# A head-norm's small gate matmuls moved one step earlier and into another PSUM bank, in a two-layer transformer kernel whose TensorE queue is written out by a planner

## The reference, cut to what matters

```
h = rms_norm(x, norm_g)
q, k, v, z = split(h @ w_in, 4)                     # 1024 x 8192
q = rms_norm(q per head and map) ; k likewise       # head 64 wide, 2 maps, 16 heads
probs   = softmax(q k^T + alibi, causal)            # for each map
weights = probs[map 0] - lam * probs[map 1]
o = weights @ v                                     # 128 columns a head
o = rms_norm(o, head_norm_g) * (1 - lam_0)          # over the 128 columns of the head
o = o.reshape(b, s, 2048) * silu(z)
return x + o @ w_out                                # 2048 x 1024
```

## Time and profile before

| | |
|---|---|
| median of 3 runs | 1321.99 us (1320.73 to 1322.24) |
| the profiled execution, its own time | 1322.24 us |
| its span, from the first to the last instruction | 1320.5 us |
| mean granted TensorE clock | 0.996 |
| TensorE matmul busy | 1303.3 us, 99% |
| VectorE, ScalarE, GpSimd busy | 794.4, 612.3, 306.7 us |
| the head loop of the second layer | from about 791 us to 1286 us |

### The profile page before, as it was taken

One profiled execution on the slowest core, in us unless ns is written; L12 is line 12 of the kernel. 1 busy time (PEld: TensorE's weight loads), 2 busy tenths in 40 slices (PEclk: granted clock), 3 DMA queues, 4 the chain that ended last, 5 costly groups with the idle time before them and its releaser, 6 DMA issues.

```text
span 1320.5 us, 18425 instructions
## 1 busy us (share of the span) xinstructions
PE 1303.3 (99%) x7206; PEld 1092.6 (83%) x7206; DVE 794.4 (60%) x1568; ACT 612.3 (46%) x1299; POOL 306.7 (23%) x206
## 2 busy tenths in 40 slices
PE   7999999999999999999999999999999999999999
PEld 6877887888889999999888787888878888888787
DVE  4416564333569788877323646576767676677643
ACT  4325555333435444445314435555555565656531
POOL 4013310000037566460001412031222223131010
PEclk8999999999999999999999999999999999999999
DMA  6303332332351442342235222222222222223501
GB/s 244 96 10 103 81 95 65 97 96 96 109 210 39 154 128 70 123 129 96 65 128 198 97 88 64 97 72 72 72 80 83 94 73 72 73 72 124 203 32 64
DMA packets 110103, 130.87 MB, mean 99 GB/s; under 512 B 7488, under 2 KB 87360, under 8 KB 110016
## 3 DMA queue, kind: packets, MB, share of 16 engines
q1 hardware_dynamic: 104400, 112.39, 26.4%
q10 hardware_dynamic: 5616, 17.30, 3.5%
HBM read 120.24 MB, written 9.44 MB: 98 GB/s over the span
## 4 chain that ended last, share of the span: by engine, by line
PE 86%; DVE 6%; issue 4%; ACT 2%; POOL 1%; DMA 0%; ACTq 0%; DVEq 0%; POOLq 0%
PE ps L811 14%; PE ps L813 14%; PE ps L812 14%; PE ps L816 7%; PE ps L818 6%; PE ps L817 6%; PE ps L1018 5%; PE ps L1021 5%; PE ps L1020 5%; PE ps L1076 2%; DVE wlo L1442 2%; PE ps L1086 1%; PE ps L1058 1%; PE ps L1110 1%; PE ps L922 1%
## 5 line engine op out<-in xcount | busy, mean ns | idle before, releaser
L1442 DVE TENSOR_TENSOR wlo<-raw,whi 128x512 fp32r<-128x512 f32 (+1 forms) x290 | 235.9, 838 | 185.1 <-ACT whi L1140 184.4
L1140 ACT ACTIVATE whi<-raw 128x512 fp32r<-128x512 f32 (+2 forms) x338 | 208.5, 650 | 116.8 <-PE ps L813 91.8
L811 PE MATMUL ps<-whi,hth 128*128 128x512 f32 x592 | 243.9, 412 | 2.6 <-DVE wlo L1442 2.6
L813 PE MATMUL ps<-wlo,hth 128*128 128x512 f32 x592 | 231.6, 391 | 0.0
L812 PE MATMUL ps<-whi,htl 128*128 128x512 f32 x592 | 231.4, 391 | 0.0
L1843 POOL TENSOR_TENSOR wlo<-raw,whi 128x384 fp32r<-128x384 f32 (+1 forms) x48 | 55.7, 1179 | 421.5 <-ACT whi L1140 421.5
L811 PEld LDWEIGHTS ps<-whi,hth 128*128 128x128 f32 x592 | 111.5, 188 | 33.6 <-issue 9.2
L813 PEld LDWEIGHTS ps<-wlo,hth 128*128 128x128 f32 x592 | 111.3, 188 | 24.7
L812 PEld LDWEIGHTS ps<-whi,htl 128*128 128x128 f32 x592 | 111.8, 189 | 18.8
L1392 ACT ACTIVATE px<-px,nm 128x128 f32<-128x128 f32 (+3 forms) x128 | 70.8, 554 | 90.4 <-DVE nm L1757 87.1
L816 PE MATMUL ps<-hth,whi 128*128 128x512 f32 (+1 forms) x288 | 112.5, 391 | 0.0
(11 more groups left out here) (339 smaller groups left out, 2872.5 us busy)
## 6 DMA issues: line engine op xcount, KB each, us to landing
raw<-in_l_w_in SPq DMA_DIRECT2D x64, 512.0 KB, 4.7
raw<-in_w_gate_up SPq DMA_DIRECT2D x44, 512.0 KB, 4.9
raw<-in_w_in SPq DMA_DIRECT2D x14, 1024.0 KB, 5.4
raw<-in_w_down SPq DMA_DIRECT2D x10, 1024.0 KB, 5.0
raw<-in_l_w_out SPq DMA_DIRECT2D x8, 1024.0 KB, 5.2
raw<-in_w_in SPq DMA_DIRECT2D x24, 256.0 KB, 3.6
raw<-in_w_branch SPq DMA_DIRECT2D x8, 512.0 KB, 4.0
raw<-in_w_out SPq DMA_DIRECT2D x4, 1024.0 KB, 5.1
```

The source lines that it names most:

```text
L811: e.matmul(o, ah, wh[:, cs], start=a, stop=False)
L813: m = e.matmul(o, ah, wl[:, cs], start=False, stop=z)
L1140: return e.activation(out, in_, ACT.Copy, **how)
L1442: return e.tensor_tensor(out, src, hi_part.bitcast(F32), ALU.subtract)
```

## The change

The gate is one step now, `ga`, for all three engines. It is put one planner step earlier, behind `t2` part 0 in place of around `t2` part 1, and writes at column 0 of `b0`, the first score bank of the slot (`gate2(b)`); in slot 16 and at the end it takes a bank of its own. The bank is free after `hvar_d`, and the bank of `t2` part 1 no longer waits for it. On VectorE the reading of the sums follows the low half of `t2` part 0. The heads that wait for their gate stand in a list, `og_wait`. In `last_heads`, slot 16 starts two steps earlier and the gate of head 15 one step earlier, with its `to` where it was; the four loads of `xb` are put together, ahead of the third step of slot 15, and three of them (the first among them) wait for `og` of head 13 (`og_p` at 14). The last projection waits once for all of its four heads.

```diff
@@ -312,6 +312,7 @@
         self.block_end(1, W.dn + 10, gen, (2, 4))
         finish(gen)
         put("ab", 0)
+        self.og_wait = []
         for g in range(7):
             merge(self.proj2(g + 1), 32, self.slots(2 * g, 2 * g + 2), 14)
         merge(self.w2_first(), 48, self.last_heads(), 28)
@@ -454,26 +455,28 @@
                     self.put("vz", g, tb)
                 yield
 
+    def gate2(self, b=None):
+        if self.og_wait:
+            self.put("ga", self.og_wait.pop(), self.bank() if b is None else b, 0)
+
     def slot(self, h):
         put = self.put
         now, last, out = h < H2, 1 <= h <= H2, 2 <= h
+        b = None
         if now:
-            put("s2", h, 0, self.bank(), self.bank())
+            b = self.bank()
+            put("s2", h, 0, b, self.bank())
             yield
         if last:
             put("t2", h - 1, 0, self.bank())
+        self.gate2(b)
         yield
         if now:
             put("cb", h, 0)
             if h + 1 < H2:
                 put("ab", h + 1)
         if last:
-            b = self.bank()
-            if out:
-                put("ga", h - 2, b, 3 * P)
-            put("t2", h - 1, 1, b)
-            if out:
-                put("gb", h - 2, b, 3 * P)
+            put("t2", h - 1, 1, self.bank())
             yield
         if now:
             put("s2", h, 1, self.bank(), self.bank())
@@ -490,6 +493,7 @@
             yield
         if last:
             put("p2", h - 1, self.bank())
+            self.og_wait.append(h - 1)
         if now:
             put("cb", h, 3)
         if last:
@@ -501,22 +505,18 @@
 
     def last_heads(self):
         yield from self.slot(14)
-        self.put("xb", (0, 1, 3))
         last = self.slot(15)
-        for _ in range(3):
+        for _ in range(2):
             next(last)
             yield
-        self.put("xb", (2,))
+        self.put("xb")
         yield from last
+        yield from self.slot(16)
         yield
         yield
-        yield from self.slot(16)
-        yield
-        b = self.bank()
-        self.put("ga", 15, b, 0)
-        self.put("gb", 15, b, 0)
-        yield
-        yield
+        self.gate2()
+        for _ in range(3):
+            yield
         self.put("to", 15, self.bank())
         yield
 
@@ -1086,7 +1086,7 @@
                         m = e.transpose(ps[b][:, P * c:P * c + P],
                                         px[2 * (h % 2)][:, QSEG[qb] + P * kb:QSEG[qb] + P * kb + P], ident[:])
                     m.then_inc(t2_pe, 1)
-                    free[b] = [(pt2_lo, 3 * h + i + 1)] + ([(hvar_d, h)] if i == 1 and h >= 1 else [])
+                    free[b] = [(pt2_lo, 3 * h + i + 1)]
                 elif kind == "p2":
                     h, b = a
                     g, vc = h // 2, slice(P * (h % 2), P * (h % 2) + P)
@@ -1109,6 +1109,7 @@
                     for qb in range(TB):
                         m = e.matmul(ps[b][:, c + qb:c + qb + 1], osq[:, P * qb:P * qb + P], ones[:, 0:1], start=True, stop=True)
                     m.then_inc(ss_pe, 1)
+                    free[b] = [(hvar_d, h + 1)]
                 elif kind == "to":
                     h, b = a
                     claim(b)
@@ -1120,11 +1121,11 @@
                 elif kind == "w2":
                     c, k, tb, i0 = a
                     b = (PJ, HI4)[c][tb] if k == 3 else PJ[tb]
-                    if k == 3:
-                        pe.wait_ge(ot_lo, i0 + 2)
                     if i0 == 0:
                         if k < 3:
                             pe.wait_ge(lod, order.lo[W.ot[k], 3])
+                        else:
+                            pe.wait_ge(ot_lo, 4)
                         if k in (0, 3):
                             claim(b)
                     three(W.w2[c, k], ps[b][:, :], 0, True, OTH, OTL, 4 * k, slice(P * tb, P * tb + P), k in (0, 3),
@@ -1423,15 +1424,14 @@
                             act.wait_ge(qt_pe, 32)
                         copy(OTH(h), ots[h % 2][:]).then_inc(ot_hi, 1)
                 elif kind == "xb":
-                    for tb in a[0]:
+                    for tb in range(TB):
                         for q in range(TB):
                             act.wait_ge(x_out[q], 32)
                         if tb == 3:
                             act.wait_ge(qt_pe, 32)
-                        elif tb == 2:
-                            act.wait_ge(og_p, 14)
                         else:
                             act.wait_ge(p2_pe, 14)
+                            act.wait_ge(og_p, 14)
                         e.dma_start(xo[tb], x2_v[tb]).then_inc(xo_in[tb], 16)
 
         @block.vector
@@ -1777,7 +1777,7 @@
                     cs = slice(KSEG[i], KSEG[i] + n)
                     dve.wait_ge(pt2_hi, 3 * h + i + 1)
                     lower(ptl2[:, cs], ps[b][:, 0:n], pth2[:, cs]).then_inc(pt2_lo, 1)
-                elif kind == "gb":
+                elif kind == "ga":
                     h, b, c = a
                     dve.wait_ge(ss_pe, h + 1)
                     dve.wait_ge(to_pe, h)
```

## The result

The changed kernel takes 1336.27 us against 1321.88 us (medians of four executions each), which is 14.4 us more. Four are few. In all there are 18 executions of it from 1330.02 to 1338.24 us, with a median of 1333.6 us; a disturbed one of 4525.18 us, among the four, is left out here and in the ratio. The ratio goes by all 18: 1.0092, 95% interval 1.0072 to 1.0113, which is some 12 us. Its profiled execution took 1333.1 us, with a span of 1331.4 us, 10.9 us more than the one before.

What follows compares the result with a forecast made beforehand. TensorE's own queue was taken to bound the kernel (busy 1303.3 of 1320.5 us). The terms, 10.7 - 1.1 + 3.3 = 12.9 us on the profiled 1322.2 us, gave 1335 us, range 1329 to 1340.

Steps and rivals of the forecast that it cites:

- No idle time to gain, every new wait paid in full: TensorE's queue: an earlier gate gives back at most 1.1 us, and any new wait there costs its full length.
- The bank: Odd slots 3 to 13: the last q/k transposition gets `b0` and waits for `hn`, six times, 10.7 us.
- The other moves in GpSimd's queue, at 0: GpSimd: the next head's bias, now behind the gate, is wanted only a slot later, so 0.
- The place of the gate at 0: Each gate on TensorE: its 0.81 us is moved and not added, so 0.
- The og wait, 1.1 us saved: Slot 16: `og` is ready one planner step earlier, removing TensorE's wait before its transposition, 1.1 us saved.
- The loads and slot 16, 3.3 us: Last slots: late x2 loads delay VectorE, so TensorE stands 3.3 us at head 15's fourth transposition.
- The lower bound of 1.0 us for slot 16 alone: Head 15's fourth transposition: TensorE still stands 1.0 us if the load is not late at all.
- The clock at 0: TensorE's seven pauses, six of 1.8 us and one of 3.3: no clock lost, counted 0.
- The sum: Whole kernel: 10.7 - 1.1 + 3.3 = 12.9 us more than the profiled execution.
- The bank is free in time: Rival, odd slots: sums read before the last q/k transposition, the 10.7 us vanish; 1324.4 us, chance 0.09.
- The earlier og gives ScalarE its time back: Rival: ScalarE's 9.7 us of waits for `og` in six places shorten the kernel; 1311.4 us, chance 0.03.
- The clock falls at each pause: Rival: each of TensorE's seven pauses costs 1.5 us more through the clock; 1345.6 us, chance 0.05.

Runs made afterwards that it cites:

- e6: Kernel before the change, with the earlier gate in slots 14 to 16 alone; 1320.73 us against 1320.86 us, ratio 0.9992.
- e3: Changed kernel, but the gate takes a bank of its own from the rotation in every slot; 1328.47 us, ratio to before 1.0054.
- e5: Changed loop with the x2 loads at their old places, and the gate put ahead of part 0 of `t2`; 1325.12 us, ratio to before 1.0032.
- e7: Changed kernel with a bank of its own for the gate and the x2 loads at their old places; 1321.62 us, ratio to before 1.0007.
- e1: Changed head loop, with the last slots, x2 loads and last projection's wait as before the change; 1330.92 us, ratio to before 1.0068.
- e4: Changed kernel with the x2 loads, and what they wait for, as before the change; 1330.64 us, ratio to before 1.0073.
- e8: Changed kernel with x2 loads at their new place, ordered 0, 1, 3, 2, only the last waiting for `og`; 1333.58 us, ratio to before 1.0094.
- e10: The changed kernel itself, run once more; 1334.3 us, ratio to before 1.0087.

## Why the prediction was right, point by point

- **No idle time to gain, every new wait paid in full.** Right. ScalarE's 9.7 us came back as other waits of ScalarE, and the best kernel, e6, gained 1.2 us from the head loop on.
- **The bank.** Right in place, count and cause: slots 3, 5, 7, 9, 11 and 13, released by `hn`. e3 removes it and e5 halves the wait. The term was sized 1.80 us each, 10.7 us in all; it measured 8.3 us, 1.38 us each. Two parts of the sum were off. I let `hn` start 0.69 us after the low half, by the record's length, where it starts after 0.60 us. And VectorE follows TensorE more closely in the changed loop: its low half starts 3.23 us after the transposition of p (1066.28 to 1069.51), not 3.59 us (1063.62 to 1067.21 before). In e7, without any bank wait, it is 3.24 us, so the waits don't cause this. I had written that the two engines would stand to each other as before. The hand-over that I allowed 0.2 us for takes 0.05 us.
- **The other moves in GpSimd's queue, at 0.** Wrong, and this is where most of the 0.36 us come from. Before the change GpSimd made the next head's bias (`ab`) at the start of each odd slot, beside VectorE's last `px`. With the gate ahead of it in the queue it makes the bias 10 us later (1072.54 in slot 9, which starts at 1062.07). First before, then changed, in slot 9:

```profile
1059.48 1.50 POOL L1895 TENSOR_SCALAR ab<-tab 128x512 f32<-128x512 f32 x1
1059.57 1.07 DVE L1773 SCALAR_TENSOR_TENSOR px<-px,rl 128x512 f32<-128x512 f32 x1 [0.79 <-ACT px L1140]
```

```profile
1062.17 0.75 DVE L1773 SCALAR_TENSOR_TENSOR px<-px,rl 128x512 f32<-128x512 f32 x1 [0.79 <-ACT px L1141]
```

This `px` took 0.96 to 1.07 us beside the bias in the six odd slots before, and 0.75 us in the six of the changed kernel and of e7. The next `px` of the same form, with no bias beside it, takes 0.75 us before the change too. So in most of these slots VectorE needed 0.32 us less ahead of the low half; if all of it reached the low half, the six waits were about 1.8 us shorter for it. No run moved the bias alone.
- **The place of the gate at 0.** Wrong by 1.1 us over twelve slots, in every slot (e3, e7): 0.06 or 0.07 us in slot 2 and the odd slots, 0.12 us in the other even ones.
- **The og wait, 1.1 us saved.** Right; with it the last slots of e1, e4, e5 and e7 are 1.4 us shorter and those of e6 1.2 us.
- **The loads and slot 16, 3.3 us.** Right in its sum, less so in its parts: e4 takes 5.06 us from the changed kernel's last slots, of which 1.7 us are clock, so 3.4 us. VectorE's wait was forecast at 4.3 us and measured 4.7 us, and its last `px` came 2.1 us late (51.64 against 49.51 us after the scores of slot 14), 2.3 us forecast. But TensorE's stand for it was forecast at 3.3 us and recorded at 2.13 us. By the projection matmuls of e4 and of the changed kernel side by side, 2.6 us are lost at this pause and 0.85 us before it, at a later part of the transposition of head 14 (the 0.26 us for `ptl` are on the list) and in its product with v, which the forecast did not have. The lower bound of 1.0 us for slot 16 alone was wrong: together with the earlier gate it is 0 (e4), since I kept the delay by `og` in the case without a late load. And the reason that I gave, the wait for `og`, is only one of two: e8 shows that the same place is late by the DMA engines' load as well.
- **The clock at 0.** Wrong for one pause of seven, right for six. The fall cost 1.7 us in two traces of the changed kernel and 3.4 us in e3 and e8. As a rival I had priced it at every pause, and it had a chance of 0.05; what happened lies between: the long pause alone, at 1.5 us forecast for a fall and 1.7 us measured. That it fell at all isn't certain in each execution, as the pause at 430 us and the execution of 1330.04 us show.
- **The sum.** 8.3 + 1.1 - 1.4 + 3.4 + 1.7 = 13.1 us by these parts, 12.9 us by the traces, 12.9 us forecast. The exact agreement is luck: the bank was 2.4 us too dear, and place and clock, 2.8 us together, stood at nothing. Without the fall the same trace would have given some 11 us, with a longer one 14.6 us. The median of four, 14.4 us more, comes from three of the slower executions; by the median of all 18 the change costs 11.7 us. The timed executions leave no trace that could show which falls each of them had.
- **The rivals.** *The bank is free in time*: no, in any slot. *The earlier og gives ScalarE its time back*: ScalarE's wait went, and TensorE got no faster for it. *The clock falls at each pause*: it fell behind none of the six short ones.

## What to carry to other kernels

When a small write is moved into another buffer of a rotation, ask who is dealt that buffer next and what stands ahead of its reader in the reader's queue: four columns of PSUM cost 1.4 us each time here, and only where the rotation met a q/k transposition. Ask the same of every other engine whose order changes: a bias that GpSimd makes at another moment changed what VectorE needed beside it. A load that is moved behind a step is late by what it waits for and by what has filled the DMA engines meanwhile; look for the first instruction that wants it in an ordered queue, and move that one load first. Where one engine is busy 99% of the span, count the waits of that engine before hoping for anything from the others.

## What the runs showed of the hardware

I had not expected one pause to cost so differently. Behind the same 2.8 us between two transpositions the granted clock was at its 1.2 GHz level for some 3.4 us in two traces (changed and e10, from about 2 us behind the pause's end) and for some 6.8 us in two others (e3 and e8, from its end on): 1.7 and 3.4 us lost. Behind a pause of the same recorded length in the first layer it fell in four traces of twelve.

VectorE's `px` of 128x512 took 0.96 to 1.07 us with a GpSimd instruction of 128x512 beside it and 0.75 us without. And the start of a gate comes 0.43 us after that of the four transpositions ahead of it, where a projection matmul comes after 0.35 us; no list of waits shows this.
